# Attention B in steps of two units: scores four ahead, and values also kept one grid row on

## What is computed

```python
def first_block(x, norm_gain, w_in, q_norm_a, k_norm_a, na_rpb, w_out, final_norm_gain):
    ...
        q_a, k_a, v_a, g_a, q_b, k_b, v_b, g_b = jnp.split(proj, split_at, axis=-1)
        ...
        o_a = _gqa_blocked(q_a, k_a, v_a) * jax.nn.silu(g_a)
        o_b = _neighbourhood_attn(q_b..., k_b..., v_b..., na_rpb[l])
        o_b = o_b * jax.nn.silu(g_b)
        x = x + jnp.concatenate([o_a, o_b], axis=-1) @ w_out[l]
    return _rmsnorm(x, final_norm_gain)

def row_block(args):                     # of _neighbourhood_attn, one grid row r
    r0 = jnp.clip(r - kh // 2, 0, rows - kh)       # kh = 8 rows of keys, rows = 16
    ...
    sc = jnp.einsum('bjqhd,bkjchd->bhjqkc', qb, k_band).astype(jnp.float32) * scale
    sc = jnp.where(mask, sc + bias.astype(jnp.float32), -jnp.inf)
    p = jax.nn.softmax(sc, axis=(-2, -1)).astype(v.dtype)
    o = jnp.einsum('bhjqkc,bkjchd->bjqhd', p, v_band)
```

## Time and profile before

| what | us |
|---|---|
| median of 3 runs | 1524.84 |
| lowest and highest | 1521.74 and 1530.44 |
| the profiled execution | 1525.87 |
| its span | 1524.1 |
| of the span: TensorE busy | 1469.4 (96%) |
| DVE, ACT, POOL busy | 800.7, 626.9, 413.3 |

### The profile page before, as it was taken

One profiled execution on the slowest core, in us unless ns is written; L12 is line 12 of the kernel. 1 busy time (PEld: TensorE's weight loads), 2 busy tenths in 40 slices (PEclk: granted clock), 3 DMA queues, 4 the chain that ended last, 5 costly groups with the idle time before them and its releaser, 6 DMA issues.

```text
span 1524.1 us, 31223 instructions
## 1 busy us (share of the span) xinstructions
PE 1469.4 (96%) x12826; PEld 1286.2 (84%) x12826; DVE 800.7 (53%) x1493; ACT 626.9 (41%) x1297; POOL 413.3 (27%) x509
## 2 busy tenths in 40 slices
PE   6999999989999999999999999999998998999998
PEld 6999998868888777778799999888897887888887
DVE  5239311158888767645440705342423776888531
ACT  5323121047777567642342212342325553777210
POOL 0212132100000166632212211121104775344420
PEclk9999999999999999999999999999997999999999
DMA  8313222000000113246423335533121011322332
GB/s 253 54 53 101 97 77 90 1 2 1 1 1 1 50 63 70 59 139 181 129 42 40 56 79 90 74 55 56 28 63 43 24 39 55 98 66 75 102 125 83
DMA packets 84517, 103.55 MB, mean 68 GB/s; under 512 B 25424, under 2 KB 68592, under 8 KB 84377
## 3 DMA queue, kind: packets, MB, share of 16 engines
q1 hardware_dynamic: 84376, 101.56, 25.7%
HBM read 78.40 MB, written 23.12 MB: 67 GB/s over the span
## 4 chain that ended last, share of the span: by engine, by line
PE 52%; DVE 4%; ACT 2%; issue 1%; POOL 0%; DVEq 0%; ACTq 0%
PE s_ps L368 22%; PE s_ps L1297 12%; PE s_ps L2750 2%; PE s_ps L2736 2%; PE s_ps L2725 1%; PE s_ps L2166 1%; PE s_ps L1123 1%; PE s_ps L1104 1%; PE s_ps L2109 1%; PE s_ps L2124 1%; PE s_ps L2713 1%; PE s_ps L2726 1%; PE s_ps L1283 1%; PE s_ps L1674 1%; DVE conv_y L1870 1%
## 5 line engine op out<-in xcount | busy, mean ns | idle before, releaser
L334 POOL TENSOR_TENSOR p_w_lo<-p_w_raw,p_w_hi 128x2048 fp32r<-128x2048 f32 (+1 forms) x27 | 126.7, 4694 | 512.1 <-ACT p_w_hi L318 512.1
L368 PE MATMUL s_ps<-p_w_hi,w_out_hi 128*128 128x256 f32 (+1 forms) x640 | 181.9, 284 | 0.1
L368 PE MATMUL s_ps<-p_w_hi,w_out_lo 128*128 128x256 f32 (+1 forms) x640 | 179.7, 281 | 0.0
L368 PE MATMUL s_ps<-p_w_lo,w_out_hi 128*128 128x256 f32 (+1 forms) x640 | 179.6, 281 | 0.0
L368 PE MATMUL f_ps<-p_w_hi,hT_hi 128*128 128x256 f32 x576 | 164.1, 285 | 1.4 <-DVE hT_lo L140 1.4
L368 PE MATMUL f_ps<-p_w_hi,hT_lo 128*128 128x256 f32 x576 | 162.9, 283 | 0.0
L368 PE MATMUL f_ps<-p_w_lo,hT_hi 128*128 128x256 f32 x576 | 162.9, 283 | 0.0
L368 PEld LDWEIGHTS s_ps<-p_w_hi,w_out_hi 128*128 128x128 f32 x640 | 120.6, 188 | 0.9 <-issue 0.6
L368 PEld LDWEIGHTS s_ps<-p_w_lo,w_out_hi 128*128 128x128 f32 x640 | 120.8, 189 | 0.0
L368 PEld LDWEIGHTS s_ps<-p_w_hi,w_out_lo 128*128 128x128 f32 x640 | 120.6, 188 | 0.0
L368 PEld LDWEIGHTS f_ps<-p_w_hi,hT_hi 128*128 128x128 f32 x576 | 109.4, 190 | 1.8 <-DVE hT_lo L140 1.8
(11 more groups left out here) (296 smaller groups left out, 3625.0 us busy)
## 6 DMA issues: line engine op xcount, KB each, us to landing
p_w_raw<-w_in SPq DMA_DIRECT2D x26, 1024.0 KB, 8.3
s_gate<-p_spill SPq DMA_DIRECT2D x48, 128.0 KB, 1.8
kbT<-x SPq DMA_DIRECT2D x8, 512.0 KB, 6.9
b_w_raw<-w_out SPq DMA_DIRECT2D x8, 512.0 KB, 4.7
qT<-s_gate SPq DMA_DIRECT2D x8, 512.0 KB, 6.8
qT<-x SPq DMA_DIRECT2D x8, 512.0 KB, 3.4
s_x<-qT SPq DMA_DIRECT2D x8, 512.0 KB, 2.6
c_table<-s_line SPq DMA_DIRECT2D x8, 512.0 KB, 3.7
```

What stands on the lines that cost most here:

```text
L334: ops.tensor_tensor(self.w_lo[:, c % 2, :, 0:w], self.raw[:, :, 0:w], self.w_hi[:, c % 2, :, 0:w].bitcast(F32), ALU.subtract).then_inc(sel ...
L368: last = self.nc.tensor.matmul(out, lhs, rhs, start=(kt == 0 and i == 0), stop=(kt == KT - 1 and i == 2))
```

## The change

Three edits that belong together. The values are kept a second time, shifted by one grid row (`v_odd`, 7 tiles per pair of heads, two pairs at a time), so that a window that begins on an odd row also is four tiles; `value_tile` chooses. The loop goes in steps of two units, with the order values of u - 2 and u - 1, turns of u and u + 1, scores of u + 4 and u + 5; scores have four banks and `prob` four slots. All four turned tiles of a unit lie in one bank, which one engine empties with one copy of 512 columns: DVE for units with u % 4 == 3, ACT for the others. The zero margins of `prob` and the POOL instruction that cleared them go; `kk`, the keys of attention A, moves in SBUF and leaves its place to `prob`.

```diff
@@ stage_first
+        with ExitStack() as pt_ctx:
+            aside = Kit(nc, pt_ctx, clears=False, side="right")
+            g.kk = aside.sb("kk", [P, A_KV, SEQ], F32R)
+            pt_aside = [aside.sb(f"a_pt_{n}", [P, NT, 4 * P], F32R) for n in ("hi1", "lo1", "hi2", "lo2")]
...
@@ NearFront
+        self.prob = k.sb("b_prob", [P, 4, self.W])
...
-        self.prob = k.sb("b_prob", [P, 2, self.W + 2 * GRID_W])
-        self.prob_t = k.sb("b_prob_t", [P, 2, 5 * P])
+        self.prob_t = k.sb("b_prob_t", [P, 2, self.W])
...
-        self.nc.gpsimd.memset(self.prob[:, :, :], 0.0)
@@ neighbourhood_part
+    v_odd = k.sb("b_v_odd", [P, 2, NT - 1, P])
+    v_odd_loaded = k.sems("b_v_odd_loaded", 2)
...
+    def emptier(u):
+        return "dve" if u % 4 == 3 else "act"
...
+    def value_tile(p, i, r0, j):
+
+        if r0 % 2:
+            return v_odd[:, p % 2, r0 // 2 + j, i * HD:(i + 1) * HD]
+        return v[:, r0 // 2 + j, (2 * p + i) * HD:(2 * p + i + 1) * HD]
+
+    def load_odd(sp, p):
+        src = g.vb[GRID_W:SEQ - GRID_W, p * P:(p + 1) * P].rearrange("(t p) c -> p t c", p=P)
+        sp.dma_start(v_odd[:, p % 2, :, :], src).then_inc(v_odd_loaded[p % 2], 16)
...
     def sync(sp):
+        load_odd(sp, 0)
+        load_odd(sp, 1)
         for kt in range(4):
             ws.load(sp, kt)
...
             if p < PAIRS - 1:
                 send(sp, p, 0, ROWS)
+            if p + 2 < PAIRS:
+                load_odd(sp, p + 2)
...
-            if u >= 2:
-                pe.wait_ge(max_ready, u - 1)
+            if u >= 4:
+                pe.wait_ge(max_ready, u - 3)
...
         def turn_probs(u):
-            _, _, tiles, c0 = window(units[u][1])
             pe.wait_ge(prob_ready, u + 1)
-            if u >= 2:
-                pe.wait_ge(pt_first_ready, u - 1)
-                wait_second(pe, u - 2)
-            for j in range(tiles):
...
+            for j in range(4):
+                last = nc.tensor.transpose(ps[:, 4 + u % 2, j * P:(j + 1) * P], prob[:, u % 4, j * P:(j + 1) * P], g.ident[:, :])
+            last.then_inc(turned, 1)
 
         def values(u):
...
+            wait_emptied(pe, u)
             if u == 0:
                 pe.wait_ge(v_loaded, 16)
+            if r0 % 2:
+                pe.wait_ge(v_odd_loaded[p % 2], 16 * (p // 2 + 1))
             if u >= 2:
                 pe.wait_ge(out_stored, 2 * (u - 1))
-            for j in range(tiles):
+            for j in range(4):
...
-        scores(0)
-        scores(1)
-        for u in range(n_units):
+        for u in range(4):
+            scores(u)
+        for u in range(0, n_units, 2):
+            if u >= 2:
+                values(u - 2)
+                values(u - 1)
             turn_probs(u)
-            if u + 2 < n_units:
-                scores(u + 2)
-            if u >= 1:
-                values(u - 1)
+            turn_probs(u + 1)
+            if u + 4 < n_units:
+                scores(u + 4)
+                scores(u + 5)
         pe.wait_ge(max_ready, n_units)
         op.turn(pe, 0)
+        values(n_units - 2)
         values(n_units - 1)
...
@@ neighbourhood_part, vector
+        for u in range(4):
+            bias_and_max(u)
+        for u in range(0, n_units, 2):
+            if u >= 2:
+                store(u - 2)
+                store(u - 1)
             if u % ROWS == 4 and u // ROWS + 1 < PAIRS:
                 keys_low(u // ROWS + 1)
-            if u % 6 == 5 and u // 6 < KT:
+            if u % 6 == 4 and u // 6 < KT:
                 ws.split_lo(dve, nc.vector, u // 6)
...
+            if emptier(u + 1) == "dve":
+                empty(u + 1)
+            if u + 4 < n_units:
+                bias_and_max(u + 4)
+                bias_and_max(u + 5)
...
@@ neighbourhood_part, scalar
+        def empty(u):
+            act.wait_ge(turned, u + 1)
             if u >= 2:
                 act.wait_ge(out_ready, u - 1)
...
+            nc.scalar.copy(prob_t[:, u % 2, :], ps[:, 4 + u % 2, :]).then_inc(pt_by["act"], 1)
...
-        for u in range(n_units):
+        for u in range(0, n_units, 2):
             if u % ROWS == 2 and u // ROWS + 1 < PAIRS:
                 keys_high(u // ROWS + 1)
-            if u % 6 == 3 and u // 6 < KT:
+            if u % 6 == 2 and u // 6 < KT:
                 ws.split_hi(act, nc.scalar.copy, u // 6)
-            empty_first(u)
-            if u % 2:
-                empty_second(u)
+            empty(u)
+            if emptier(u + 1) == "act":
+                empty(u + 1)
             if u + 2 < n_units:
                 exponentials(u + 2)
+                exponentials(u + 3)
```

## The result

| what | before | after |
|---|---|---|
| median, us | 1524.28 | 1510.06 |
| lowest and highest | 1521.74 and 1530.44 | 1508.00 and 1512.58 |
| the profiled execution | 1525.87 | 1508.52 |
| its span | 1524.1 | 1506.3 |

Four runs each. The ratio is 0.9916, with a 95% interval of 0.9891 to 0.9942: 14.2 us or 0.84% faster, where 1513.5 us, 11.5 us faster, was forecast.

The account below looks back on a forecast made before the run. TensorE was taken to bound attention B. 14.1 us saved, less 1.6 (values after values) and 1.0 (loads at the start), gave 11.5 us: 1525.87 to 1514.4 profiled, median 1513.4, rounded to 1513.5; range 1509.5 to 1520.

Parts of the forecast that it names:

- The bound: Attention B, steady part: TensorE busy in all of 31.00 us; a four-tile unit's turns, scores and values cost 1.90 us.
- The fifth tile: Attention B, 16 of 64 units with odd windows: removing 16 turns and 32 value products saves 3.7 us on TensorE.
- Steps of two: TensorE in attention B, values, turns, scores (V V T T S S): a pair costs 3.48 us instead of 3.80.
- The border V to V: Between the value products of a pair's two units: 0 to 0.17 us, or 0 to 5.4 us for 32 pairs.
- the border stays inside a pair: Rival, TensorE in attention B: values after values cost 0.17 us like values to turns, giving 1517.5 us; chance 0.17.
- The waits: Between the value products of a pair's two units: satisfied waits may show, taken as 0.05 us a pair, 1.6 us.
- The other engines: DVE, ACT and POOL in attention B keep up with 3.48 us steps; added waits covered by 0.65 us or more.
- The loads at the start: Start of attention B: two transfers ahead of the weights delay ACT's cast, between 0.3 and 6 us, taken as 1.0.
- The start and the clock: Start of attention B: twelve scores at the 1.2 GHz level, 0.42 us each, put the first turn at 539.6.
- A clock that falls within the steady part: Rival, attention B: granted clock sinks, costing 2.9 us a pair; half the stage would give 1560 us; chance 0.03.
- The end: End of attention B, from unit 60's turns: last values start at 649.2 against 663.26, 14.1 us earlier.
- the likeliest case: Whole kernel: the forecast itself, 1513.5 us, 11.5 us faster, within 1510 to 1516.5; chance 0.62.

Follow-up runs that it names:

- its repetition: The changed kernel, unaltered, run again on the same chip as later runs; 1511.38 us, ratio 0.9918 to the kernel before, attention B 118.14 us.
- a step of four: The changed kernel with steps of four units (four values, four turns, four scores) instead of two; 1503.79 us, ratio 0.9872 to the kernel before.

## Why the prediction was right

*The bound.* Right. TensorE's order of work set the stage; its sum of rates and borders gave all three distances of a step to 0.03 us.

*The fifth tile.* 3.7 us forecast. The kernel with this edit alone is 3.3 us faster at equal clock (2.8 to 3.9), and nearly all its units lie 1.90 apart.

*Steps of two.* A pair was forecast at 3.48 us plus 0.05 and took 3.50. The border V to V, the one unknown on which a rival hung, is 0.02 us of the 0 to 0.17 that the rows allowed. T to T is 0, as taken. The rival "the border stays inside a pair" is refuted by the 0.46 us between the two V's. By the Trainium skill's rule in "TensorEngine Tiling (Array Packing)", section Key Properties, that a change of tiling mode drains TensorE, the term would have been 0, and that came nearer than the 0.05 that I took. The trace agrees with it: where the weights change between 128x64 and 128x128 the border is 0.16 us from V to T and from T to V and 0.10 from S to V, and it is 0.02 from V to V, where they don't. Scores and turns both have 128x128 weights, and their border still showed 0.08 in the trace of before, which that rule does not cover; so the tiling is not the whole of a border's price.

*The waits.* 0.05 us a pair was put in for them: too much. Satisfied waits cost nothing here, even six or seven of them between two V's (32 loads in 1.01 us with them). Mis-sized term: 1.5 us over 30 steps in the sum, 0.9 measured (105.27 less 104.4), of which 0.2 is the slow first step.

*The other engines.* Right: 0.65 us of cover at the second exponential was forecast and 0.69 measured; ACT never held TensorE in the steady part, and the idle time put down to it at the end, 0.9 us, was in the forecast of the end. The tightest place was not the second exponential, though, but V in the step with both casts, with some 0.3 us in hand.

*The loads at the start.* This is the step that was off in kind. I took 1.0 us between 0.3 and 6; it was 0. I had put one pair of transfers behind the other (4.7 us, then 4.7 more, so 544 to 545), as if 4.7 us were what a transfer costs the next one. In fact a transfer landed 1.2 to 1.4 us behind the one before it, and the first weights were there at 541.8. The 4.7 was also misread: it is the median of three loads, and the two at the start took 4.7 and 5.6. The second mistake went the other way: the cast was wanted at 542.24 and not at 543.7, and weights landing at 544 to 545 would have held it by some 2 us. The slack of 5.7 us in the trace of before (landed at 539.2, cast at 544.90) gave 2.7 to the earlier demand and 2.6 to the later landing; 0.45 was left.

*The start and the clock.* 5.1 us to the first T, 4.21 in the profile of after and 4.87 in its repetition. The mechanism holds; when the clock rises differs from run to run, and nothing in these traces places it beforehand. A clock that falls within the steady part was not seen: 1.00 from 541 to 572 us.

*The end.* Right to 0.08 us at every step of it, and POOL's first product was done 2.4 us before the turns, where 2.7 was forecast.

*The chances.* Two of them don't add up. Faster by more than 0.5% was given 0.77, but its parts are 0.62, half of 0.17 and half of 0.06, which is 0.735, and at most 0.02 from the rest; within 0.5% the parts make about 0.22 and not 0.19.

Together: 1.0 us from the loads and 0.6 from the pairs (105.27 against 105.9) are lasting gains that I did not grant; the 0.9 at the start is luck: the repetition has only 0.2 of it and loses 0.5 in the first step. The median of 1510.06 us lies at the very edge of the 1510 to 1516.5 that the likeliest case was given. 11.5 + 1.0 + 0.6 gives 13.1 us, against 13.0 in the trace of the repetition, 12.4 to 12.6 at equal clock, and 14.2 and 13.1 between the medians.

## What to carry to other kernels

Where TensorE alternates between short groups of products of different shape, read the distance between the first loads of neighbouring groups, take off the group's own rate, and what is left is the price of a border; grouping the same kind for several units then saves a sum that can be worked out beforehand, here to 0.02 us for a pair and 0.03 for a step of four. Check the engines that empty the banks at the tightest instruction of a step, not by their busy share, and put no price on waits that are already satisfied: between two V's they had none here. When loads are issued behind one another, take their distance from one landing to the next, not the whole time from issue to landing. And read a change inside one stage from the trace of that stage, with the clock beside it, or at equal mean clock: single runs of before lie up to 11 us apart with the clock (1518.4 to 1529.5).

## What was unexpected of the hardware

The clock at the start of attention B differs from execution to execution after the same kind of pause: its mean from 534 to 541 us was 1.00 in two traces, 0.76 in three and 0.51 to 0.56 in four. With twelve scores first, 2.65 to 4.87 us passed between the first score and the first turn, and the mean clock over the span of identical programs (before) ranged from 0.987 to 0.998, which goes with 11 us of device time.

Two transfers of 448 KB in runs of 512 B and two of 512 KB, issued within 4 us, landed one every 1.2 to 1.4 us, though each took 5.2 to 6.9 us from issue to landing; in before the second of two of 512 KB landed 1.3 us behind the first. So each further transfer added 1.2 to 1.4 us to the last landing, with short runs (1.4) hardly more than with long ones.

Two groups of 16 value products into different banks, with weights of different units and up to seven waits between them, run as one: their 32 loads take 1.01 us.
